# Two reorderings at the renewal of the residual stream: high parts of k tiles 4 and 5 ahead of the second inverse norm on ScalarE, first-half sums of squares three k tiles later on TensorE

## The reference, cut to what matters

```python
def _rms(x, g):
    x32 = x.astype(jnp.float32)
    y = x32 * lax.rsqrt(jnp.mean(x32 * x32, axis=-1, keepdims=True) + EPS) * g.astype(jnp.float32)
    return y.astype(x.dtype)
...
    h = _rms(x, p['g_mix_pre'])
    proj = h @ p['w_in']
    ...
    x = x + _rms(m @ p['w_out'], p['g_mix_post'])
    f = jnp.square(jax.nn.relu(_rms(x, p['g_mlp_pre']) @ p['w_up'])) @ p['w_down']
    x = x + _rms(f, p['g_mlp_post'])
```

## Time and profile before

| | us |
|---|---|
| median of three runs | 2032.9 (2031.54 to 2036.31) |
| profiled execution | 2029.05 |
| its span | 2027.2 |
| TensorE matmuls busy | 1985.7 |
| VectorE busy | 1069.3 |
| ScalarE busy | 955.3 |
| GpSimd busy | 277.9 |

### The profile page before, as it was taken

One profiled execution on the slowest core, in us unless ns is written; L12 is line 12 of the kernel. 1 busy time (PEld: TensorE's weight loads), 2 busy tenths in 40 slices (PEclk: granted clock), 3 DMA queues, 4 the chain that ended last, 5 costly groups with the idle time before them and its releaser, 6 DMA issues.

```text
span 2027.2 us, 38778 instructions
## 1 busy us (share of the span) xinstructions
PE 1985.7 (98%) x15694; PEld 1939.5 (96%) x15694; DVE 1069.3 (53%) x1976; ACT 955.3 (47%) x1503; POOL 277.9 (14%) x302
## 2 busy tenths in 40 slices
PE   7999999999999999999999999999999999999997
PEld 7999999999999999999989999999999999999997
DVE  6657576765437432343456676757645474224334
ACT  5466656565236431332365756565732554213323
POOL 4212111100101200120041212020001012002100
PEclk9999999999999999999999999999999999999998
DMA  5323232222332232333313232322223323233322
GB/s 137 108 68 93 69 93 69 83 69 80 91 95 72 83 92 85 89 88 90 98 53 99 73 97 72 89 73 78 74 84 89 99 64 92 84 93 84 93 84 67
DMA packets 308455, 172.00 MB, mean 85 GB/s; under 512 B 7592, under 2 KB 303872, under 8 KB 308320
## 3 DMA queue, kind: packets, MB, share of 16 engines
q1 hardware_dynamic: 300768, 155.47, 26.8%
q0 software_dynamic: 7520, 14.59, 2.6%
q10 hardware_dynamic: 32, 0.04, 0.0%
HBM read 158.86 MB, written 11.21 MB: 84 GB/s over the span
## 4 chain that ended last, share of the span: by engine, by line
PE 81%; ACT 9%; DVE 6%; issue 2%; DMA 0%; SPq 0%; ACTq 0%; DVEq 0%
PE PJ L687 65%; PE PJ L699 4%; PE PJ L859 4%; PE PX L887 2%; ACT w_hi L1115 2%; DVE w_lo L1590 1%; PE PX L905 1%; PE PX L925 1%; DVE T L1701 1%; PE PX L941 1%; PE PX L699 1%; DVE uc L1831 1%; ACT L1332 1%; DVE Y L1622 1%; ACT L1145 1%
## 5 line engine op out<-in xcount | busy, mean ns | idle before, releaser
L1590 DVE TENSOR_TENSOR w_lo<-w_raw,w_hi 128x1024 fp32r<-128x1024 f32 x284 | 384.5, 1359 | 370.3 <-ACT w_hi L1115 369.6
L687 PE MATMUL PJ<-h_hi,w_hi 128*128 128x272 f32 x2304 | 490.7, 294 | 2.6 <-DVE T L1701 1.9
L687 PE MATMUL PJ<-h_hi,w_lo 128*128 128x272 f32 x2304 | 475.6, 289 | 0.0
L687 PE MATMUL PJ<-h_lo,w_hi 128*128 128x272 f32 x2304 | 474.6, 288 | 0.0
L1115 ACT ACTIVATE w_hi<-w_raw 128x1024 fp32r<-128x1024 f32 x284 | 297.8, 1051 | 234.0 <-DMA w_raw<-in_w_down 116.4
L687 PEld LDWEIGHTS PJ<-h_hi,w_hi 128*128 128x128 f32 x2304 | 360.2, 189 | 12.8 <-issue 9.5
L687 PEld LDWEIGHTS PJ<-h_lo,w_hi 128*128 128x128 f32 x2304 | 361.5, 189 | 0.0
L687 PEld LDWEIGHTS PJ<-h_hi,w_lo 128*128 128x128 f32 x2304 | 360.3, 189 | 0.0
L687 PE MATMUL PJ<-u_hi,w_hi 128*128 128x272 f32 x960 | 198.4, 288 | 0.0
L687 PE MATMUL PJ<-u_hi,w_lo 128*128 128x272 f32 x960 | 197.4, 288 | 0.0
L687 PE MATMUL PJ<-u_lo,w_hi 128*128 128x272 f32 x960 | 197.1, 287 | 0.0
(11 more groups left out here) (341 smaller groups left out, 3511.4 us busy)
## 6 DMA issues: line engine op xcount, KB each, us to landing
w_raw<-in_w_in SPq DMA_DIRECT2D x110, 512.0 KB, 3.8
w_raw<-in_w_down SPq DMA_DIRECT2D x64, 512.0 KB, 3.8
w_raw<-in_w_up SPq DMA_DIRECT2D x62, 512.0 KB, 4.2
w_raw<-in_w_branch_attn SPq DMA_DIRECT2D x16, 512.0 KB, 3.8
w_raw<-in_w_branch_lru SPq DMA_DIRECT2D x16, 512.0 KB, 3.8
w_raw<-in_w_out SPq DMA_DIRECT2D x16, 512.0 KB, 3.7
out_prompt_k<-stage POOLq DMA_DIRECT2D x16, 256.0 KB, 2.8
out_prompt_v<-GA POOLq DMA_DIRECT2D x8, 512.0 KB, 4.0
```

The costliest lines, as they stand in the source:

```text
L687: mm = pe.matmul(PJ[:, buf, half, 0:HT], w[a], src[b][:, k0 + k, HT * half:HT * half + HT], start=first and k == 0 and a + b == 0, stop=en ...
L1590: dve.tensor_tensor(low(n)[:], raw(n), w_hi[:, n.hi, :, :].bitcast(F32), ALU.subtract).then_inc(w_lo_ready, 1)
```

## The change

On TensorE, where S is even, the first half's sum of x's squares is issued behind k tile 4 of the second half of `trio` in place of k tile 1. On ScalarE, in all three renewals, the high parts of chunk 3 (k tiles 4 and 5) of the first half are made ahead of the second half's inverse norm of y in place of behind it. Nothing is added or removed.

```diff
@@ trio @@
                         if h == 0 and k == 1 and S > 0:
                             y_half_sum((S - 1) // 2, (S - 1) % 2, 1)
-                        if h == 1 and S % 2 == 0 and k == 1:
+                        if h == 1 and S % 2 == 0 and k == 4:
                             x_sums(l, 0, (0, 1), 3)
                         if h == 1 and S % 2 == 0 and k == 6:
                             x_sums(l, 1, (0, 1), 1, stop=False)
@@ renew, ScalarE @@
                 h_chunk(S, 0, 2)
                 split_hi(mlp_tile(l, 0, 0, 2) if s == 0 else pair_tile(l + 1, 0, 2))
+                h_chunk(S, 0, 3)
                 y_rs_half(l, s, 1)
-                h_chunk(S, 0, 3)
                 h_chunk(S, 0, 4)
                 if s == 1:
                     for c in range(5):
```

## The result

The kernel after took 2036.95 us (median of 20 runs, 2033.48 to 2038.67), the kernel before, on the same occasions, 2032.85 (median of 20, 2029.97 to 2036.9). The ratio is 1.0017 with a 95% interval of 1.0011 to 1.0023: 4.1 us by the medians, 3.5 by the ratio, 2.2 to 4.7 by its interval. Its profiled execution, at 2033.48 the fastest of the 20, has a span of 2031.7, against 2027.2.

A forecast was written before the change was run, and what follows sets the result against it. TensorE's matmuls were taken to bound the kernel, filling 98% of the span, with its waits left to win or lose. -0.64 + 2.34 + 1.6 = +3.3 on the median 2032.9 gave 2036.2 us, range 2032.4 to 2040.2.

The forecast's parts named there:

- High parts ahead, renewals 1 and 3: ScalarE's earlier high parts let TensorE start k tile 4 0.32 us earlier in each; together -0.64, bounds 0 and -1.6.
- the wait for k tile 4 falls by 0.3: Expected sign in renewals 1 and 3: TensorE waits 0.3 us less there, with no new wait in the second half.
- just in time: Second half of renewal 1: k tile 2's low part would end at 635.85, and TensorE would want it at 635.92.
- High parts ahead, renewal 2: ScalarE's squares start 0.2 us late, so k tile 2 of the second half starts 0.21 later on TensorE.
- Sums later, the wait: Renewal 2: ScalarE's Ln waits for TensorE's moved sums, delaying k tile 6 by 2.34 us; bounds 1.0 and 2.9.
- The clock: Renewal 2's second half: TensorE's emptied stall lets its clock fall, doubling 13 matmuls; +1.6 us, bounds 0 and 5.6.
- the first rival: Renewal 2's second half: k tiles 2 to 4 and the sums all at 1.2 GHz, costing 4.0; 2038.6 us, chance 0.38.
- the longer fall: The clock falls for all of k tiles 2 to 4 and the sums in renewal 2; 2038.6 us, chance 0.38.
- a second fall: One more fall of TensorE's clock behind the long wait for k tile 6 in renewal 2, priced at 1.6 us.
- No fall: Rival: the clock holds in renewal 2's second half and only the wait counts; +1.7, 2034.6 us, chance 0.15.
- Faster: Rival: clock falls in the three first halves go away, 4.8 us back, Ln's wait covered; 2027.5 us, chance 0.04.
- The start (S = 0): The sums move here too, but would be ready 2.8 us before they are needed; cost 0.

The follow-up runs named there:

- e1: The kernel before with only ScalarE's edit, the high parts of chunk 3 ahead of the second inverse norm; 0.9995 of the kernel before.
- e7: The kernel after with unread matmuls of ones in renewal 2's second half, four behind k tile 1 and three behind k tile 5; 1.0005 of the kernel before.
- e3: The kernel before with the first half's sums behind k tile 2 in place of k tile 1; 1.0 of the kernel before, 0.9993 in a second series.
- e6: The kernel before with high parts ahead in renewals 1 and 3 only, and Ln and Exp behind k tiles 6 and 7; 0.9988, then 0.998 of the kernel before.
- r8: The kernel after, unchanged, run once more for a second trace; 2037.19 us in one run.
- e4: The kernel after with four unread matmuls of ones behind k tile 1 of renewal 2's second half; 1.0014 of the kernel before.

## Why the prediction was right, point by point

- **High parts ahead, renewals 1 and 3.** The sign "the wait for k tile 4 falls by 0.3" can't be read from the two traces as they stand (0.70, then 1.60), because the clock fell in one and not in the other. K tile 4 itself came 0.33 earlier against the renewal's first matmul (627.04 - 619.22 against 627.63 - 619.48), as worked out. The term was -0.32 each and came out as -0.22: the "just in time" of k tile 2 in the second half wasn't quite. Its low part ended at 635.11 + 0.48 = 635.59, TensorE started on it at 635.65, and the restart made this k tile 1.17 long in place of 1.06.
- **High parts ahead, renewal 2.** Forecast 0.2 late; e1 has 0.20.
- **Sums later, the wait.** Forecast +2.34; with the clock held, e7 has +2.33. The page and the busy times alone would have called this edit free: its matmuls moved from one stall to another. The price came from who waits for their result, and from what is queued behind that waiter.
- **The clock.** The fall was forecast at its place, between k tiles 1 and 5. The term was mis-sized: +1.6 was taken for 13 matmuls, from the fall of the earlier trace rows, and 5.60 - 3.30 = +2.3 was measured. As to length, the first rival was nearer: the fall took nearly all 27 matmuls and not 13. As to price, both put a matmul's time at double (0.12 more), and it rose from 0.12 to 0.21. The two errors of the forecast went opposite ways and in part cancelled, which was luck. The rival's 4.0 counted the sums in too, and these ran behind the fall.
- **Sum.** -0.64 + 2.34 + 1.6 = +3.3 was forecast, -0.44 + 4.65 = +4.2 is in the trace, +4.1 in the medians. That the last two agree to 0.1 is luck in part: differences of 1.0 and 1.5 us stand elsewhere in the traces, and for e3 and e6 trace and medians are up to 2.5 us apart. The forecast of 2036.2 stands 0.75 below the measured 2036.95. The chance of 0.57 for less than 0.2% goes with a median change of just 0.2%; the interval, 0.11% to 0.23%, leaves that open too.
- **The range.** Its upper end, 2040.2, is the longer fall's 2038.6 and 1.6, which is the whole of a second fall and not a part of it.
- **The rivals.** No fall: e7 shows what it would have been, and it isn't what the kernel after does. Faster: renewal 2's first-half fall didn't go away with the edit. Its price was wrong too: renewal 1 of the kernel after took 28.29 without a first-half fall, and 28.30 in the second trace (r8), which had one. There TensorE waits for k tile 4 either way (1.60 and 0.23 us), and the fall only takes up part of the wait. The start (S = 0): its fourth weight tile begins between 41.95 and 44.85 us in the six traces with the sums behind k tile 4, and between 42.35 and 44.95 in the five with them behind k tile 1. So no loss shows there, though a loss under 1 us could hide in that spread.

## What to carry to other kernels

Before an operation is moved into a later idle gap of its engine, look up who waits for its result, and what stands behind that waiter in its queue. A small operation in a gap may also be what keeps TensorE's clock up: with the gap emptied, the matmuls that followed cost as much again here (2.3 us beside a wait of 2.3). Where a long chain such as Ln and Exp with two table loads stands ahead of short work that TensorE needs sooner, try the short work first.

## What was not expected of the hardware

- A fall of the granted clock can be moved, not only removed: with one stall filled (e4) it came behind the next, at 0.68 over 5.40 us.
- Falls also come where nothing changed, and not in every trace. These stretches, 82 to 88 us behind renewal 2's fourth weight tile, hold the same work in both kernels. In the kernel after it ran at 0.72, and the time from renewal 2's fourth weight tile to renewal 3 was 573.02 there, against 571.52 before.

```profile
1127.00:1133.00 6.00, 6.00 (x37) 0.72 0.30 87
```

```profile
1122.80:1128.80 6.00, 6.00 (x50) 1.00 0.31 90
```

The first is of the kernel after, the second of the kernel before. The second trace of the kernel before has 572.97 between the same two points. Ahead of renewal 1 the traces differ still more: its count begins between 613.86 and 619.17 us, with no relation to the edit that shows. Chance falls like this one may well explain part of the spread of 7 us between runs of one kernel, though this wasn't shown run by run. All this is why the lengths of the renewals are the better measure of an edit of this size.
